# Conformer/DeltaNet trunk on one core: twelve unread TensorE products around each stage's closing row

## The reference, cut to what matters

```python
for l in range(DEPTH):                                  # DEPTH = 2
    h = swiglu_ffn(rms_norm(x, ffn1_norm_pre[l]), ffn1_w_in[l], ffn1_w_out[l])
    x = x + 0.5 * rms_norm(h, ffn1_norm_post[l])        # stage 0
    h = rms_norm(x, mix_norm_pre[l]) @ mix_w_in[l]
    o_gdn = gated_deltanet_group(h, ...)
    o_cm = conformer_conv_group(h, ...)
    h = jnp.concatenate([o_gdn, o_cm], axis=-1) @ mix_w_out[l]
    x = x + rms_norm(h, mix_norm_post[l])               # stage 1, the mixer
    h = swiglu_ffn(rms_norm(x, ffn2_norm_pre[l]), ffn2_w_in[l], ffn2_w_out[l])
    x = x + 0.5 * rms_norm(h, ffn2_norm_post[l])        # stage 2
    x = rms_norm(x, block_norm[l])
```

## Time and profile before

| | |
|---|---|
| median of 3 runs | 2178.27 us (2178.06 to 2178.55) |
| profiled execution, its time | 2178.44 us |
| profiled execution, its span | 2176.7 us |
| PE busy | 2101.3 us, 97% of the span |
| DVE busy | 1220.5 us, 56% |
| ACT busy | 715.4 us, 33% |
| mean granted TensorE clock | 0.972 of full speed |

### The profile page before, as it was taken

How to read it: one execution, slowest core, us unless ns; L and a number is a source line. 1 busy time by engine, 2 the same in 40 slices (tenths; PEclk the granted TensorE clock), 3 DMA queues, 4 the chain that set the end, 5 groups by cost and what they waited for, 6 DMA issues and landing times.

```text
span 2176.7 us, 26239 instructions
## 1 busy us (share of the span) xinstructions
PE 2101.3 (97%) x10024; PEld 1753.7 (81%) x10024; DVE 1220.5 (56%) x1683; ACT 715.4 (33%) x982; POOL 24.4 (1%) x39
## 2 busy tenths in 40 slices
PE   7999999999989999999999999999999899999997
PEld 6888888778977888888788888877888678888886
DVE  5555422888893755532475554358878756555323
ACT  4222222444434422222242222233533443222222
POOL 1000000000010000000000000000000100000000
PEclk9999999999999999999999999999989999999997
DMA  5333333220013233333233333323200123333320
GB/s 153 114 96 96 90 98 99 71 78 20 20 39 87 78 97 96 96 97 98 76 97 96 96 94 90 97 68 97 68 20 20 39 68 114 96 97 94 90 80 39
DMA packets 345792, 177.54 MB, mean 82 GB/s; under 512 B 8338, under 2 KB 344692, under 8 KB 345716
## 3 DMA queue, kind: packets, MB, share of 16 engines
q1 hardware_dynamic: 344058, 176.34, 28.3%
q10 hardware_dynamic: 1658, 0.16, 0.1%
HBM read 174.38 MB, written 2.10 MB: 81 GB/s over the span
## 4 chain that ended last, share of the span: by engine, by line
PE 88%; DVE 8%; ACT 2%; issue 1%; DMA 0%; SPq 0%; DVEq 0%; ACTq 0%
PE res L466 24%; PE res L467 24%; PE res L468 24%; DVE u L1429 2%; PE pq L732 2%; PE pq L741 1%; PE res L530 1%; PE res L531 1%; PE pq L466 1%; PE res L534 1%; PE pq L468 1%; PE pq L467 1%; PE stat L473 1%; PE bc L494 1%; PE stat L634 1%
## 5 line engine op out<-in xcount | busy, mean ns | idle before, releaser
L890 ACT ACTIVATE wh<-raw 128x1024 fp32r<-128x1024 f32 (+1 forms) x336 | 348.6, 1040 | 1031.7 <-PE res L468 1010.5
L466 PE MATMUL res<-xh,wh 128*128 128x512 f32 x1576 | 621.0, 394 | 4.6 <-ACT Um L1122 2.3
L1265 DVE TENSOR_TENSOR wl<-raw,wh 128x1024 fp32r<-128x1024 f32 (+1 forms) x336 | 402.5, 1200 | 381.1 <-ACT wh L890 381.1
L467 PE MATMUL res<-xl,wh 128*128 128x512 f32 x1576 | 615.8, 391 | 0.0
L468 PE MATMUL res<-xh,wl 128*128 128x512 f32 x1576 | 615.7, 391 | 0.0
L466 PEld LDWEIGHTS res<-xh,wh 128*128 128x128 f32 x1576 | 297.7, 189 | 66.5 <-ACT Um L1122 2.7
L468 PEld LDWEIGHTS res<-xh,wl 128*128 128x128 f32 x1576 | 297.3, 189 | 62.3
L467 PEld LDWEIGHTS res<-xl,wh 128*128 128x128 f32 x1576 | 297.7, 189 | 61.1 <-issue 0.5
L466 PE MATMUL res<-hh,wh 128*128 128x512 f32 x704 | 273.9, 389 | 0.0
L467 PE MATMUL res<-hl,wh 128*128 128x512 f32 x704 | 273.9, 389 | 0.0
L468 PE MATMUL res<-hh,wl 128*128 128x512 f32 x704 | 273.9, 389 | 0.0
(11 more groups left out here) (286 smaller groups left out, 1940.1 us busy)
## 6 DMA issues: line engine op xcount, KB each, us to landing
raw<-in_ffn_w_in SPq DMA_DIRECT2D x176, 512.0 KB, 3.8
raw<-in_ffn_w_out SPq DMA_DIRECT2D x64, 448.0 KB, 3.7
raw<-in_mix_w_in SPq DMA_DIRECT2D x48, 512.0 KB, 3.9
raw<-in_ffn_w_out SPq DMA_DIRECT2D x32, 512.0 KB, 3.9
raw<-in_mix_w_out SPq DMA_DIRECT2D x16, 512.0 KB, 3.9
xin<-in_x SPq DMA_DIRECT2D x4, 512.0 KB, 5.1
out_dram<-xin SPq DMA_DIRECT2D x4, 512.0 KB, 4.0
crows<-in_cm_dw_w ACTq DMA_DIRECT2D x1, 62.0 KB
```

Of the source, the lines that this page charges most:

```text
L466: pe.matmul(bank, wh[:, slot, j, :], hi, start=first, stop=False)
L467: pe.matmul(bank, wh[:, slot, j, :], lo, start=False, stop=False)
L890: act.activation(wh[:, slot, 0:nk, :], raw[:, slot, 0:nk, :], ACT.Copy).then_inc(hi_full, 1)
L1265: dve.tensor_tensor(wl[:, slot, 0:nk, :], raw[:, slot, 0:nk, :], wh[:, slot, 0:nk, :].bitcast(F32), ALU.subtract).then_inc(lo_full, 1)
```

## The change

Behind the sums at each stage end PE gets three products, and behind the spread of their row nine more. Each multiplies the identity by a matrix of ones, 128 by 128 by 128 columns in float32, into the first quarter of the PSUM bank `pq[:, 0, :]`, which holds nothing wanted at that time. Nobody waits for them or reads them, they wait for nothing, and they raise no semaphore. They stand behind the instruction that raises `ssq_full` and behind the one that raises `bc_full`.

```diff
                 token_sums(acc[:], last=False)
                 pe.wait_ge(ysq_ready, l * 3 * KD + (stage + 1) * KD)
                 token_sums(sqr[:, (KD - 1) % 2, :], first=False).then_inc(ssq_full, 1)
+                idle_products(3)
+
+            def idle_products(n):
+
+                for _ in range(n):
+                    pe.matmul(in_bank(4)[:, 0:P], ident[:], ones[:], start=True, stop=True)
 
             def spread_column(col):
...
                 if q == 1 and l == 0:
                     pe.wait_ge(s_cc, S_CC)
                 spread_column(rmix if q == 2 else rcol).then_inc(bc_full, 1)
+                if q % 2:
+                    idle_products(9)
```

## The result

The changed kernel takes 2183.01 us in the median of 19 runs (2172.82 to 2187.23). The kernel before, run beside it, takes 2176.57 us in the median of 19 (2161.65 to 2179.40). The ratio is 1.0040, with a 95% interval of 1.0025 to 1.0055 (it is worked out over all runs; the quotient of the two medians is 1.0030): slower by 0.3 to 0.4%. Forecast was 2177.4 us in a range of 2172.4 to 2182.4, which is 0.9 us less than before; the medians differ by 6.4 us the other way.

The account below looks back on a forecast made before the run. PE, busy in 97% of the span, was taken to bound the kernel through its waits and clock. A gain of 4.9 us less 4.0 us for falls gave -0.9 us: 2177.4 us, range 2172.4 to 2182.4 us.

Parts of the forecast that it names:

- What bounds the kernel: Whole kernel: PE is busy in 97% of the span, so time comes only from its waits or its speed.
- Three and nine products fit and hold the clock at the ends: Six stage ends: products fit PE's gaps, pushing the spread at most 0.1 us each (0 taken); full clock holds.
- 4.9 us gained: Stage ends held at full clock: 1.7 us from faster spreads plus 3.2 us from ACT's shorter waits.
- PE's wait at the sums of x grows to 2.2 us: Ahead of the sums of x, PE arrives earlier; its wait for DVE grows from 0.35 to about 2.2 us.
- I take two or three falls of 1.6 us: Behind four sums of x: half clock gives back 4.0 us, within bounds of 0 to 6.8 us.
- The 0 for layer 1's first stage: Layer 1's first stage: the existing fall stays; its longer wait costs 0 to 1.7 us more, taken as 0.
- The nearest row that I named: Layer 1's first stage before: 1.57 us wait plus two 0.9 us sums, 3.4 us in all, then half clock.
- The base and its range: Kernel before: profiled 2178.44 us, 0.17 us over the median, three runs within 0.5 us; forecast range 2172.4 to 2182.4 us.
- Rival (c): Layer 0's mixer: its chain of small products falls to half clock, price 4.8 us, giving 2182.2 us; chance 0.12.
- Rival (d): Stage ends: clock falls anyway, first product 1.9 us late in five ends, +9 us, 2187 us; chance 0.05.
- Rival (a): Sums of x: clock holds there too, nothing is given back, -4.9 us, 2173.4 us; chance 0.14.

Follow-up runs that it names:

- The kernels with filled mixers: Idle products at three places in each mixer (10, 3 and 10), on the kernel before: 2165.60 us; on the changed kernel: 2168.45 us.
- the kernel with eighteen products: The changed kernel with 18 idle products instead of 9 behind the spread: 2166.83 us, ratio 0.9969 to the kernel before.

## Why the prediction was wrong, point by point

*What bounds the kernel* held: the time came and went with the clock and PE's waits.

*Three and nine products fit and hold the clock at the ends*: right in the trace after at all six ends. The push of the spread was 0.05 us at the first end, where 0 was taken.

*4.9 us gained*: right, 5.4 us, each of its six places within 0.15 us, and cut at ACT's wait as said (27.86 us from the first end to its sums, also with 18 products). Not all of it comes at the sums of x, as the prediction has it: 0.3 us of it is the output's.

*PE's wait at the sums of x grows to 2.2 us*: 1.96 us; 3.08 us in layer 1's first stage where "some 3" was said.

*"I take two or three falls of 1.6 us"*: this step failed: the term of 2.5 x 1.6 = 4.0 us for four sums of x. The 0 for layer 1's first stage held in the trace after (342.66 against 342.68 us), though three other traces had a fall of 6.7 us there. In the traces of all kernels there are 23 sums of x with a wait of 1.84 to 3.10 us, and 22 of them have a fall. There are 29 in all kernels' traces with a wait of at most 0.5 us (layer 1's first stage left out), and none falls. Layer 1's first stage, with its two sums, fell in five of six traces at waits of 1.45 to 1.73 us, and in one of two at waits under 0.2 us. The nearest row that I named, 1.57 us of wait with two sums, pointed to "falls", and I still halved it. The price was right for a short fall (341.29 to 342.87 us, 1.58 us) but its upper bound was not: ten of the 22 are 6.7 us long, and such a one costs a feed-forward stage 3.2 us. In the trace after these falls and what else moved behind the sums of x cost 9.0 us, where 4.0 were taken. The kernels with filled mixers show the same balance with less noise: stage by stage their two traces have 1.6 us lost in each of two feed-forward stages, 3.2 us in the last, nothing in the mixers (the fall at layer 0's sums of x is paid by a shorter one at the 32 one-column products), 6.3 us in all, against 5.3 us gained. The 1.0 us between them is most of the 1.3 us by which the two spans differ.

*The base and its range*: three runs within 0.5 us were taken to show that the kernel does not vary. With 19 runs it went from 2161.65 to 2179.40 us, with a median 1.7 us lower. So the change was missed by 7.3 us (6.4 slower, 0.9 faster forecast), more than the 5.6 us between forecast and measured time. Of these 7.3 us the two traces show 3.8 (2.9 and 0.9); what the others are is not shown. The Trainium skill (TensorE: Matmul & The Clock Gate, Part 1) states that the watch over PE runs free, so that the point at which the clock changes moves from run to run; I weighed this and set it aside. These runs agree with it: one kernel's mean clock went from 0.970 to 0.982, and around the same wait of 2.3 us near the start the clock falls in one trace and not in the other. The trace before had the mixers at 298.3 us in layer 1 and 292.3 in layer 0, and the kernel with eighteen products shows 290.0 and 290.7 us with the same work in them; a range that took the kernel's own spread in had to be wider.

*Rival (c), layer 0's mixer gets the long stretch*: it came, in the trace after (535.5 to 549.0) and in three others. Of the 5.1 us there 1.5 us is the fall at the sums of x (289.20 us with it against 287.66 without, mixers filled), and the other 3.6 us is what is left: the long stretch, less the pieces near 478 and 526 us that became shorter or went. The price of 4.8 us was read over a stretch that held layer 0's longer fall at its stage end (10.1 against 6.7 us); from the sums of x to the end the two mixers before differ by 6.05 us (298.31 - 292.26). Whether the changed kernel takes it oftener than before can't be said from one trace each; the times hint at it: 4 of the 19 runs of before lie below 2168 us, the fastest of the changed kernel's 19 is 2172.82. This part stays open.

*Rival (d)*: its price was wrong. It counted a first product that is 1.9 us late as 1.9 us lost; the kernel with eighteen shows, at full clock, 1.5 us of lateness at no cost. At half clock no run shows it.

*Rival (a)*, no fall at the sums of x, did not happen. Filling them by hand made it true in the trace, and the feed-forward stages had the lengths that it needs (341.3 us). In the time it can be neither confirmed nor refuted: the ratio's interval is 6.1 us faster to 2.2 us slower, and 4.9 us faster lies within it.

## What to carry to other kernels

A filled wait ahead of a joint only moves the wait to the joint: before you fill one gap with idle products, compute how long the engine then waits at the next place, and what stands behind that place. Count one-column products as part of the gap. Fill waits where full-rate work without slack follows, or let the engine come late where another engine sets the time: eighteen products here beat nine. And take the spread of a kernel's runs before its median; a few runs that agree don't show that it is steady.

## What the runs showed of the hardware

The mean clock does not tell the time of two different kernels: the changed kernel ran at a mean clock of 0.979 and took 2181.30 us in its profiled run, the kernel before at 0.972 took 2178.44, and runs of before at 0.979 took 2164.2 to 2166.3 us. A fall at a stage end cost 0.5 to 2.0 us for 6.7 to 10.1 us at half clock, since PE waits there anyway; one behind the sums of x of a feed-forward stage cost its full half (1.6 us for 3.3, 3.2 us for 6.7).

Three products, 0.7 us of work between two waits, were enough, in the one trace of that kernel, to keep full clock at three of five ends, where it had been lost at all five. Thirty-two one-column products without any wait were enough to lose it in 22 of 24 mixers.

The mixer's chain of small products (64 columns, then 128) stayed at half clock for 13.5 us in each of the 12 mixers in which it fell, and the same products kept full clock in the other 12. 23 idle products a mixer, 5 us of PE's time, came with no long stretch in six mixers of six, and with less run-to-run spread: 5.2 us in ten runs with the mixers filled, 2.3 us in six with the sums of x filled as well, against 16 to 20 us before.
